# A decoder layer's opening: 22 products of a cleared tile, the first x tile pass by pass, and another order of VectorE's work in the key jobs

## What is computed

```
h = jnp.einsum('bsd,de->bse', x, w_in[l]) + b_in[l]
qa, ka, va, qb, kb, vb, qc, z = jnp.split(h, split_idx, axis=-1)
oa = banded_causal_attention(rope(qa), rope(ka), va, 127, sinks)
ob = dilated_attention(rope(qb), rope(kb), vb)
mk, mv = jnp.split(jnp.einsum('bmd,de->bme', mem, w_mem[l]), 2, axis=-1)
oc = memory_attention(qc, mk, mv)
y = concat(rms(oa), rms(ob), rms(oc)) * g_branch[l] * silu(z)
x = layer_norm(alpha * x + y @ w_out[l])
```

## Time and profile before

| | |
|---|---|
| Time, median of 3 runs | 506.56 us (505.66 to 507.02) |
| Profiled execution | 505.63 us |
| Its span, first to last instruction | 503.2 us |
| TensorE busy | 488.2 us, 97% |
| VectorE busy | 311.3 us, 62% |
| ScalarE busy | 226.7 us, 45% |
| Granted clock, mean | 0.996 |
| Mean DMA rate | 135 GB/s |

### The profile page before, as it was taken

How to read it: one execution, slowest core, us unless ns; L and a number is a source line. 1 busy time by engine, 2 the same in 40 slices (tenths; PEclk the granted TensorE clock), 3 DMA queues, 4 the chain that set the end, 5 groups by cost and what they waited for, 6 DMA issues and landing times.

```text
span 503.2 us, 9750 instructions
## 1 busy us (share of the span) xinstructions
PE 488.2 (97%) x3504; PEld 447.8 (89%) x3504; DVE 311.3 (62%) x893; ACT 226.7 (45%) x511; POOL 70.4 (14%) x51
## 2 busy tenths in 40 slices
PE   4999999999999999999999999999999999999994
PEld 4999999999999988888888888898888888888883
DVE  4776645557574853434544468876767868777634
ACT  5632123112121134564546669947374656454540
POOL 0000000000000000111011100023232323231414
PEclk9999999999999999999999999999999999999998
DMA  8966272538632244433321347823342424241022
GB/s 283 377 181 188 95 241 83 171 122 268 203 121 104 95 144 139 117 106 92 101 96 41 103 162 247 252 56 105 113 135 68 137 64 152 64 144 52 1 83 85
DMA packets 51710, 67.83 MB, mean 135 GB/s; under 512 B 9552, under 2 KB 41168, under 8 KB 51664
## 3 DMA queue, kind: packets, MB, share of 16 engines
q1 hardware_dynamic: 51088, 66.17, 41.5%
q10 hardware_dynamic: 576, 1.05, 0.6%
HBM read 51.18 MB, written 16.02 MB: 134 GB/s over the span
## 4 chain that ended last, share of the span: by engine, by line
PE 87%; DVE 4%; SPq 3%; DMA 2%; ACT 2%; issue 1%; DVEq 0%; ACTq 0%
PE long_ps L959 16%; PE o_ps L917 10%; PE wide L780 8%; PE wide L782 8%; PE wide L781 8%; PE narrow L897 5%; PE long_ps L857 5%; PE wide L885 5%; PE long_ps L859 5%; PE long_ps L858 5%; PE wide L886 4%; DMA mem_raw<-in_mem_t 2%; SPq L584 1%; PE narrow L935 1%; SPq L588 1%; PE wide L792 1%
## 5 line engine op out<-in xcount | busy, mean ns | idle before, releaser
L780 PE MATMUL wide<-x_hi,w_hi 128*128 128x256 f32 x320 | 89.8, 280 | 0.3 <-DVE w_lo L1194 0.3
L782 PE MATMUL wide<-x_hi,w_lo 128*128 128x256 f32 x320 | 89.3, 279 | 0.0
L781 PE MATMUL wide<-x_lo,w_hi 128*128 128x256 f32 x320 | 89.3, 279 | 0.0
L780 PEld LDWEIGHTS wide<-x_hi,w_hi 128*128 128x128 f32 x320 | 60.1, 188 | 0.5 <-issue 0.4
L782 PEld LDWEIGHTS wide<-x_hi,w_lo 128*128 128x128 f32 x320 | 60.2, 188 | 0.0
L781 PEld LDWEIGHTS wide<-x_lo,w_hi 128*128 128x128 f32 x320 | 59.8, 187 | 0.0
L1040 ACT ACTIVATE spill<-turn 128x512 fp32r<-128x512 f32 x21 | 13.3, 632 | 103.3 <-DVE turn L1276 76.6
L1548 POOL TENSOR_TENSOR g_lo<-g_raw,g_hi 128x1024 fp32r<-128x1024 f32 x6 | 14.3, 2387 | 272.3 <-ACT g_hi L1045 272.3
L959 PE MATMUL long_ps<-wo_hi,y_hi 128*128 128x512 f32 (+1 forms) x128 | 52.2, 408 | 0.0
L959 PE MATMUL long_ps<-wo_lo,y_hi 128*128 128x512 f32 (+1 forms) x128 | 51.4, 402 | 0.0
L959 PE MATMUL long_ps<-wo_hi,y_lo 128*128 128x512 f32 (+1 forms) x128 | 50.8, 397 | 0.0
(11 more groups left out here) (168 smaller groups left out, 1232.9 us busy)
## 6 DMA issues: line engine op xcount, KB each, us to landing
q_spill<-spill SPq DMA_DIRECT2D x32, 256.0 KB, 2.5
q_pair<-q_spill SPq DMA_DIRECT2D x128, 64.0 KB, 2.0
w_raw<-in_w_qkv SPq DMA_DIRECT2D x12, 512.0 KB, 5.0
x_raw<-in_x_t SPq DMA_DIRECT2D x16, 256.0 KB, 8.1
g_raw<-in_w_gate SPq DMA_DIRECT2D x8, 512.0 KB, 3.6
q_pair<-q_spill SPq DMA_DIRECT2D x32, 128.0 KB, 2.8
q_pair<-q_spill SPq DMA_DIRECT2D x128, 32.0 KB, 1.8
wo_raw<-in_w_out SPq DMA_DIRECT2D x8, 512.0 KB, 4.4
```

The source lines that it names most:

```text
L780: pe.matmul(dst, w_hi[s][:, k, f], t_hi[:, k, cols], start=(k == 0), stop=False)
L781: pe.matmul(dst, w_hi[s][:, k, f], t_lo[:, k, cols], start=False, stop=False)
L782: mm = pe.matmul(dst, w_lo[s][:, k, f], t_hi[:, k, cols], start=False, stop=(k == KT - 1))
```

## The change

**TensorE.** Before the first chunk, once GpSimd has cleared 384 columns of `square_out` (semaphore `cleared`), TensorE runs 22 products of 128x128 by 256 columns of that tile into `wide0`, which nobody reads. Then comes tile 0 in a function of its own, `first_tile`: for each half of the tokens, four high-high products, four with the weights' low part and four with x's low part. The waits stand at the passes: the low part of x is waited for ahead of the third pass. The tiles 1 to 7 are as before.

```diff
--- before.py
+++ after.py
@@ -106,7 +106,9 @@
 
 GATE_ITERATIONS = 2
 FIRST_PIECES = ((0, 1), (1, 2), (2, 4), (4, 8))
-PREPARED = {3: (4, (5, 6, 6, 7)), 4: (8, (9, 9, 10, 10)), 5: (11, (11, 11, 12, 12)), 6: (13, (13, 13, 14, 14)),
+MEMORY_AT = (1, 2, 3, 4)
+WARM_UP = 22
+PREPARED = {3: (4, (5, 6, 6, 7)), 4: (8, (8, 9, 9, 10)), 5: (11, (11, 11, 12, 12)), 6: (13, (13, 13, 14, 14)),
             7: (18, (18, 19, 19, 20)), 8: (22, (22, 23, 23, 24)), "g0": (26, (27, 27)), "g1": (27, (28, 28))}
 QS = 4
 QUERIES_AT = 28
@@ -336,6 +338,7 @@
         gate_full, x_used, out_full = sem("gate_full"), sem("x_used"), sem("out_full")
         narrow_read = [sem(f"narrow_read{b}") for b in range(2)]
 
+        cleared = sem("cleared")
         x_rounded, chunk_rounded, chunk_split = sem("x_rounded"), sem("chunk_rounded"), sem("chunk_split")
         x_split, first_rounded, first_split = sem("x_split"), sem("first_rounded"), sem("first_split")
         first_full, first_read = sem("first_full"), sem("first_read")
@@ -735,10 +738,34 @@
 
         @block.tensor
         def _(pe):
+            def first_tile():
+
+                s = slot_of(0)
+                pe.wait_ge(first_rounded, 1)
+                for h in range(2):
+                    blocks = range(h * NB // 2, (h + 1) * NB // 2)
+                    pe.wait_ge(x_rounded, h + 1)
+                    for i in blocks:
+                        pe.matmul(first_ps[i // 2][:, (i % 2) * C:(i % 2 + 1) * C], x_hi[:, 0, i * P:(i + 1) * P],
+                                  w_hi[s][:, 0, :], start=(i % 2 == 0), stop=False, skip_group_check=True)
+                    if h == 0:
+                        pe.wait_ge(first_split, 1)
+                    for i in blocks:
+                        pe.matmul(first_ps[i // 2][:, (i % 2) * C:(i % 2 + 1) * C], x_hi[:, 0, i * P:(i + 1) * P],
+                                  w_lo[s][:, 0, :], start=False, stop=False, skip_group_check=True)
+                    pe.wait_ge(x_split, h + 1)
+                    for i in blocks:
+                        pe.matmul(first_ps[i // 2][:, (i % 2) * C:(i % 2 + 1) * C], x_lo[:, 0, i * P:(i + 1) * P],
+                                  w_hi[s][:, 0, :], start=False, stop=False, skip_group_check=True)
+
             def first_chunk():
 
                 s = slot_of(0)
-                for k in range(KT):
+                pe.wait_ge(cleared, 1)
+                for _ in range(WARM_UP):
+                    pe.matmul(wide[0][:, 0:C], square_out[:, 0:P], square_out[:, P:P + C], start=True, stop=True)
+                first_tile()
+                for k in range(1, KT):
                     for m, (lo, _) in enumerate(FIRST_PIECES):
                         if lo == k:
                             pe.wait_ge(first_rounded, m + 1)
@@ -749,8 +776,8 @@
                             pe.wait_ge(x_split, 2 * k + i // (NB // 2) + 1)
                         cols = slice(i * P, (i + 1) * P)
                         dst = first_ps[i // 2][:, (i % 2) * C:(i % 2 + 1) * C]
-                        pe.matmul(dst, x_hi[:, k, cols], w_hi[s][:, k, :], start=(k == 0 and i % 2 == 0),
-                                  stop=False, skip_group_check=True)
+                        pe.matmul(dst, x_hi[:, k, cols], w_hi[s][:, k, :], start=False, stop=False,
+                                  skip_group_check=True)
                         pe.matmul(dst, x_hi[:, k, cols], w_lo[s][:, k, :], start=False, stop=False,
                                   skip_group_check=True)
                         mm = pe.matmul(dst, x_lo[:, k, cols], w_hi[s][:, k, :], start=False, stop=(k == KT - 1),
@@ -1329,14 +1356,15 @@
                     x_lo_half(k, h)
             for q in range(4):
                 chunk_lo(1, q)
+            finish_first()
             for q in range(4):
                 chunk_lo(2, q)
-            for q in range(4):
-                memory_lo(q)
-            finish_first()
             for what, n in plan.steps:
                 {"job": finish_job, "keys": keys_lo}[what](n)
                 if what == "job":
+                    for q in range(4):
+                        if MEMORY_AT[q] == n:
+                            memory_lo(q)
                     for item, q in plan.split_after(n):
                         if item in ("g0", "g1"):
                             first_gate_lo(int(item[1]), q)
@@ -1548,6 +1576,7 @@
                 pool.tensor_tensor(g_lo[f % 2][:, :, :], g_raw[f % 2][:, :, :], f32(g_hi[f % 2][:, :, :]),
                                    ALU.subtract).then_inc(gate_split, 1)
 
+            pool.memset(square_out[:, 0:P + C], 0.0).then_inc(cleared, 1)
             for v in (v_a, v_b, v_c):
                 pool.memset(v[:, :, :, HD:VW], 1.0).then_inc(ones_set, 1)
             for v in range(ITERATIONS):
```

## The result

Over six executions beside six of the kernel before, the changed kernel took 502.87 us in the median (501.92 to 503.5) against 505.99 us (505.41 to 507.02). The ratio is 0.9934, with a 95% interval of 0.992 to 0.9949: faster by 0.7%. The forecast was 502.7 us. Two single executions lie far above all others and enter no ratio, one of 694.57 us with another order of passes and one of 2110.18 us with three tiles pass by pass; no run shows why.

The account below looks back on a forecast made before the run. TensorE, busy for 97% of the span, was taken as the bound. Gains of 1.97 (opening), 1.06 (first keys) and 0.43 us (chunk 4) sum to 3.46, giving 502.2 or 503.1; the middle, 502.7 us, was forecast, range 501.6 to 504.6.

Parts of the forecast that it names:

- What bounds the kernel: Whole kernel: TensorE, busy for 97% of the span, stays the bound, so the 3.46 us shift reaches the end.
- The start of the real work: Opening: tile 0's first real product at 6.00, tile 1's second half at 10.98, TensorE beginning near 1.35.
- dear-product rival: Warm-up: bf16 products cost as much as plain f32 ones, making the kernel slower, 507.8 to 508.8 us; chance 0.04.
- after that 12 + 144 = 156 products follow: 17.70 us, to 28.68: First chunk from 10.98: remaining products run 0.1135 us apart, so the first key job starts at 28.68, not 30.65.
- The opening's term: Opening through the first chunk: warm clock and tile 0 pass by pass gain 1.97 us by the first key job.
- The stop at the keys: First keys' transposition: VectorE reading first banks sooner removes TensorE's wait for the rotation, 1.06 us, margin 0.4 us.
- Chunk 4's: After the memory values: moving low-part quarters earlier removes TensorE's wait for w_lo, 0.43 us, bounds 0.2 to 0.43.
- The rival in which these waits come back: Keys and chunk 4: margins of 0.4 and 0.2 us fail, TensorE waits as before, 504.0 to 504.6 us; chance 0.06.
- The clock: Opening: TensorE's clock rises about 4.46 us after the first cleared product; the warm-up ends at 6.05.
- the middle between 502.2 and 503.1: Forecast total: 502.7 us, between profile-based and median-based times, since the kernel before may vary with the clock's rise.
- a cold clock: Opening: cleared products don't lift the clock, tile 0 starts at half clock, 503.4 to 504.4 us; chance 0.08.
- a clock that falls back in the pauses: Pauses at 8.8 and 10.5: clock drops again, the opening gains nothing, 504.2 to 505.2 us; chance 0.07.

Follow-up runs that it names:

- order_only: The kernel before with VectorE's new order and mem's quarters behind jobs 1 to 4, opening and table unchanged: 505.02 us, ratio 0.9984.
- opening_only: The changed TensorE opening with VectorE's order and the table of the kernel before: 505.63 us, ratio 1.0003.

## Why the prediction came out

**What bounds the kernel** held: TensorE was busy for 98% of the span, and what was won ahead of 67 us was won at the end but for 0.2 us. On the way 0.4 us of the lead went at one place, the transfer of queries that stands in the list of waits:

```profile
322.06 0.39 PE L912 MATMUL wide<-k_a,q_pair 128*128 128x256 f32 x1 [0.22 <-DMA q_pair<-q_spill]
```

The changed kernel's second profile doesn't have this wait, so it isn't in every execution of the kernel.

**The start of the real work** held: 6.12 for 6.00, the second half of tile 1 at 11.03 for 10.98. The clear took 0.42 us and TensorE began at 1.21 (1.35). The bf16 products cost what the fp32r rows said, 0.2133 us at half clock, so the dear-product rival is out. The Trainium skill ("TensorE: Matmul & The Clock Gate", section "Wait — 56ns, not 53.3ns?") gives for bf16 the columns divided by 1.2 GHz at the slow clock and divided by 2.4 GHz plus about 2.5 ns at the fast one, so 213 and 109 ns for 256 columns. The trace agrees at both: 213.3 ns before the rise, 109 after.

**The step that failed** is "after that 12 + 144 = 156 products follow: 17.70 us, to 28.68". It took the 0.1135 of the earlier trace rows for the pace of this stage. That was one of two paces which this stage can have: 0.74 us there and another 0.21 in the two key jobs, with 0.05 from the later start the 1.0 us missing. The opening's term measured 1.18 us, not 1.97. The trace of before held the warning, outside the rows that I took: its window from 70 to 170 us, shown above, has 851 products of the same shape in 100 us, 0.1175 each. I read a single stretch of 24 us.

**The stop at the keys** held: it went, by the order of VectorE's work, with 0.9 us of margin for the 0.4 forecast, since TensorE came later. The order_only and opening_only runs show more than the sum could: 1.97 and 1.06 are no independent terms. Without the second the first is worth nothing. **Chunk 4's** 0.43 us held. The quarters of mem are hidden, and would be nearly so in one piece. The rival in which these waits come back didn't occur.

**The clock** held in the part that mattered. It rose between 2.8 and 5.5 us after the first cleared product in the eleven profiles with them, a wider spread than the half microsecond quoted in the prediction. In the changed kernel it was 3.2 us where 4.46 was forecast, so the warm-up ended near 5.2 and TensorE stood 0.8 us until ScalarE delivered; nothing in tile 1's start depended on that. The other use of it failed: I took the middle between 502.2 and 503.1 because the kernel before should vary with the clock's rise. Its further executions moved its median down, from 506.56 to 505.99, and not for that reason that any run shows. How near the total came is luck in part. Between the two profiled executions the time fell 2.5 us (505.63 to 503.12), 1.0 us short of the 3.5 forecast; between the medians it fell 3.1 us, since the profile of before lay 0.4 us under its median and that of the changed kernel 0.25 us above its own. No run shows why. The starting point that the middle implies, 506.1, was within 0.2 us of the measured 505.99. The rivals with a cold clock or a clock that falls back in the pauses didn't occur: behind each pause the spacing was 0.113 or 0.118, never 0.214.

**What stays open** is what chooses the pace. Neither stops, nor the products' type, nor the order of passes, nor a transposition ahead decides it. Each of these trials rests on one profile: that refutes a rule without exceptions, but a shift of the odds would not show. In the long stage 113.4 is rare (one profile of 14), in the first chunk without cleared products it was there in three of three, and with them in four of eleven. The four are two with one tile pass by pass and both with three, so its share with cleared products may depend on what follows them; two against two is no proof. The comparisons ran on three chips, and on each of them the first chunk showed both paces, so the chip alone doesn't decide it either. The weight loads show where the 4.4 ns lie, but not why. In both profiles of the kernel with three tiles a load in the window from 70 to 170 us takes 188 ns in the mean and starts 3 ns behind a product; the next product starts 110 ns behind that load at the one pace and 115 at the other.

## What to carry to other kernels

When a stop sits behind the stage that you speed up, find what releases it. If the chain comes from a transfer and another engine's queue, the gain ends there, and both edits must be made together to be worth anything. Asking for each operand only at the pass that reads it let TensorE start 0.7 us sooner (5.97 for 6.69), and can be carried to more tiles than the first, where three instead of one gave another 0.7 to 1.0 us; warming the clock gave 0.2 to 1.25 us by the first keys, and how much depends on the pace that the execution has. And count products in a window before you take a pace from one stretch: with two paces 4% apart, the same stage of the same program differs by 4 us between executions.

## What the runs showed of the hardware

- At the full granted clock, 1.00 in every window, products of 128x128 by 256 columns of fp32r start either 113.4 or 117.8 ns apart. Either pace holds over hundreds of products (947 and 946 in a row), through changes of tile, bank and job, and the same program takes the one in one execution and the other in the next. In the key jobs, between the transpositions, both occur in one execution: in the changed kernel's profile 113.4 from 39.0 to 41.0 us and 117.7 from 44.5 to 47.1. Cleared fp32r products started 120.0 ns apart.
- The execution at 113.4 ns in the long stage took 497.2 us, its neighbours 501.1 to 501.4. The kernel before has a group of times at 501.1 to 502.3 beside its usual 505.2 to 507.7; that these are executions with the long stage at 113.4 would fit the 4.2 us, but no profile of one exists.
- The granted-clock column reads 1.00 in the first microseconds, too, while products are 0.2133 us apart; the spacing of like products is the safer view of the clock at the start.
- Cleared products of bf16 raise the clock like others: 0.2133 us apart at first, 0.109 after the rise.
